# The last memory value slab behind the mixer's output, and the weight splits around the norms

## What is computed

```python
def first_block(x, mem, ...):
    for l in range(DEPTH):                       # DEPTH = 2
        a = hybrid_mixer(rms_norm(x, pre_mix_g[l]), positions, rel_bias, w_in[l], ..., w_mix_out[l])
        x = x + rms_norm(a, post_mix_g[l])
        c = memory_cross_attention(rms_norm(x, pre_xattn_g[l]), rms_norm(mem, mem_g[l]),
                                   w_xq[l], w_xk[l], w_xv[l], w_xo[l])
        x = x + rms_norm(c, post_xattn_g[l])
        hdn = jnp.square(jax.nn.relu(rms_norm(x, pre_mlp_g[l]) @ w_up[l]))
        x = x + rms_norm(hdn @ w_down[l], post_mlp_g[l])
    return x
```

## Time and profile before

| | us |
|---|---|
| median of three runs | 1433.41 |
| lowest and highest | 1430.36, 1434.37 |
| the profiled execution | 1432.31 |
| its span in the trace | 1430.5 |
| TensorE busy | 1352.4 (95%) |
| VectorE busy | 826.6 (58%) |
| ScalarE busy | 661.4 (46%) |

### The profile page before, as it was taken

How to read it: one execution, slowest core, us unless ns; L and a number is a source line. 1 busy time by engine, 2 the same in 40 slices (tenths; PEclk the granted TensorE clock), 3 DMA queues, 4 the chain that set the end, 5 groups by cost and what they waited for, 6 DMA issues and landing times.

```text
span 1430.5 us, 23851 instructions
## 1 busy us (share of the span) xinstructions
PE 1352.4 (95%) x10479; PEld 1298.9 (91%) x10479; DVE 826.6 (58%) x874; ACT 661.4 (46%) x934; POOL 85.3 (6%) x65
## 2 busy tenths in 40 slices
PE   4998999999999999899999999999989998999998
PEld 3997988989999999798898999999888897899998
DVE  5467436566654475743665665437848765666542
ACT  4354435455544444543444554434445544455432
POOL 3000002020000000000202000001100100000000
PEclk7999999999999999999999999999989999999999
DMA  6724234334655533414434365555333122356553
GB/s 190 222 77 148 81 126 148 118 118 147 196 188 189 184 119 93 147 52 155 148 98 138 121 204 183 200 189 150 118 125 119 52 96 89 99 172 200 179 195 101
DMA packets 195574, 202.94 MB, mean 142 GB/s; under 512 B 5716, under 2 KB 191847, under 8 KB 195471
## 3 DMA queue, kind: packets, MB, share of 16 engines
q1 hardware_dynamic: 192704, 194.82, 42.1%
q0 software_dynamic: 2464, 5.99, 1.5%
q10 hardware_dynamic: 303, 0.61, 0.1%
HBM read 200.33 MB, written 3.16 MB: 142 GB/s over the span
## 4 chain that ended last, share of the span: by engine, by line
PE 76%; DVE 11%; ACT 8%; issue 3%; DMA 2%; POOL 0%; ACTq 0%; DVEq 0%; POOLq 0%
PE bank L561 13%; PE bank L562 13%; PE bank L563 13%; PE bank L2083 6%; PE bank L2085 6%; PE bank L2087 6%; DVE w_lo L525 4%; ACT w_hi L515 3%; PE bank L602 2%; PE bank L603 2%; PE bank L604 2%; DVE head_sq L1547 1%; PE bank L1945 1%; PE bank L1923 1%; PE bank L1976 1%
## 5 line engine op out<-in xcount | busy, mean ns | idle before, releaser
L525 DVE TENSOR_TENSOR w_lo<-raw,w_hi 128x2048 fp32r<-128x2048 f32 (+7 forms) x210 | 424.1, 2029 | 429.3 <-ACT w_hi L515 429.0
L515 ACT ACTIVATE w_hi<-raw 128x2048 fp32r<-128x2048 f32 (+7 forms) x210 | 354.8, 1704 | 455.0 <-PE bank L563 190.5
L561 PE MATMUL bank<-act_hi,w_hi 128*128 128x256 f32 x1096 | 312.8, 285 | 0.0
L563 PE MATMUL bank<-act_hi,w_lo 128*128 128x256 f32 x1096 | 310.1, 283 | 0.0
L562 PE MATMUL bank<-act_lo,w_hi 128*128 128x256 f32 x1096 | 310.1, 283 | 0.0
L2083 PE MATMUL bank<-h_hi,w_hi 128*128 128x256 f32 x768 | 212.2, 276 | 0.0
L2085 PE MATMUL bank<-h_lo,w_hi 128*128 128x256 f32 x768 | 212.0, 276 | 0.0
L2087 PE MATMUL bank<-h_hi,w_lo 128*128 128x256 f32 x768 | 212.0, 276 | 0.0
L561 PEld LDWEIGHTS bank<-act_hi,w_hi 128*128 128x128 f32 x1096 | 210.3, 192 | 0.6 <-DVE act_lo L1764 0.3
L562 PEld LDWEIGHTS bank<-act_lo,w_hi 128*128 128x128 f32 x1096 | 210.3, 192 | 0.3
L563 PEld LDWEIGHTS bank<-act_hi,w_lo 128*128 128x128 f32 x1096 | 210.3, 192 | 0.0
(11 more groups left out here) (333 smaller groups left out, 2265.2 us busy)
## 6 DMA issues: line engine op xcount, KB each, us to landing
raw<-in_w_up_dram SPq DMA_DIRECT2D x32, 1024.0 KB, 5.4
raw<-in_w_down_dram SPq DMA_DIRECT2D x32, 1024.0 KB, 4.8
raw<-in_w_ff_dram SPq DMA_DIRECT2D x32, 1024.0 KB, 5.3
raw<-in_w_in_dram SPq DMA_DIRECT2D x23, 1024.0 KB, 5.3
raw<-in_w_xk_dram SPq DMA_DIRECT2D x8, 1024.0 KB, 4.8
raw<-in_w_xv_dram SPq DMA_DIRECT2D x8, 1024.0 KB, 4.9
raw<-in_w_mix_out_dram SPq DMA_DIRECT2D x8, 1024.0 KB, 4.8
raw<-in_w_xq_dram SPq DMA_DIRECT2D x8, 1024.0 KB, 4.8
```

The costliest lines, as they stand in the source:

```text
L515: ins = act.activation(d, r, ACT.Copy)
L525: ins = dve.tensor_tensor(d, r, h.bitcast(F32), ALU.subtract)
L561: pe.matmul(o, stat_hi, mov_hi, start=first, stop=False)
L563: return pe.matmul(o, stat_lo, mov_hi, start=False, stop=last)
```

## The change

**The value slab.** Slabs are renumbered: 16 to 18 are values, 19 to 22 the mixer's output, and 23 is the last value slab. TensorE goes from `ot` 2 and 3 straight to mixer slab 19, of which it multiplies the upper half (k 4 to 7) first, with a wait on `o_lo` 2, then waits for `o_lo` 4 and does the lower half. Behind slab 22 the step `values` does the first 9 matmuls of slab 23 (tile 0, k 0 to 2), then comes `stat` 2, then `values_rest` with the other 39; the dummy matmuls ahead of pair 24 go from 10 to 4. ScalarE copies the bank xv3 behind the eight scaled tiles instead of ahead of the mixer's banks.

**The splits around the norms.** `branch_out` no longer splits a slab ahead of its last bank. Behind the mixer slab 25 is split between the last bank's copy and the root, and slab 26 behind the scaled tiles, on both engines. Behind the cross attention's output slab 34, and behind the down slabs slab 66, are split behind the scaled tiles. In the second block slabs 25 and 29 are split behind the scaled tiles instead of ahead of the last update of x.

The tables of sources and banks follow the numbers and are left out below, as are the callers of `half_slab` with their new last argument.

```diff
      ("slab", 16), ("turn", 9), ("pv", 8), ("turn", 10), ("pv", 9), ("slab", 17), ("turn", 11), ("pv", 10),
-     ("pv", 11), ("slab", 18), ("ot", 2), ("ot", 3), ("slab", 19)]
-    + [("slab", s) for s in range(20, 24)] + [("stat", 2), ("pair", 24), ("stat", 3), ("slab", 26),
+     ("pv", 11), ("slab", 18), ("ot", 2), ("ot", 3)]
+    + [("slab", s) for s in range(19, 23)] + [("values", 23), ("stat", 2), ("values_rest", 23), ("pair", 24), ("stat", 3), ("slab", 26),
      ("scores", 12), ("scores", 13), ("slab", 27), ("turn", 12), ("turn", 13), ("scores", 14), ("scores", 15),
...
+FIRST_VALUES = 3
+
 WARM = {("pair", 0): ("z0", 9), ("turn", 0): ("turn0", 1), ("pv", 0): ("o0", 3), ("pv", 5): ("scores6", 4),
-        ("slab", 16): ("xv0", 6), ("pv", 7): ("xv0", 2), ("pv", 11): ("xv2", 3), ("pair", 24): ("xq0", 10),
+        ("slab", 16): ("xv0", 6), ("pv", 7): ("xv0", 2), ("pv", 11): ("xv2", 3), ("pair", 24): ("xq0", 4),
         ("pair", 32): ("up0", 10), }
...
-        def half_slab(pe, layer, s, o, src_hi, src_lo, half):
+        def half_slab(pe, layer, s, o, src_hi, src_lo, half, opens):
...
                     dst = o[:, T * m:T * m + T]
-                    pe.matmul(dst, wh[:, k, c], src_hi[:, k], start=k == 0 and m == 0, stop=False, skip_group_check=True)
+                    pe.matmul(dst, wh[:, k, c], src_hi[:, k], start=opens and k == 4 * half and m == 0, stop=False, skip_group_check=True)
                     pe.matmul(dst, wh[:, k, c], src_lo[:, k], start=False, stop=False, skip_group_check=True)
-                    ins = pe.matmul(dst, wl[:, k, c], src_hi[:, k], start=False, stop=k == 7, skip_group_check=True)
-            if half:
+                    ins = pe.matmul(dst, wl[:, k, c], src_hi[:, k], start=False,
+                                    stop=not opens and k == 4 * half + 3, skip_group_check=True)
+            if not opens:
                 ins.then_inc(sig["slab_used"], 1)
...
                     for c in range(per_bank):
-                        if (s + c) + 3 <= 66:
+                        if (b, c) != (3, per_bank - 1):
                             split_hi(act, layer, s + c + 3)
...
                 split_hi(act, layer, 18)
-                for b in range(4):
-                    if b == 3:
-                        o_part(layer, 2, 0, 0)
-                        o_part(layer, 3, 0, 1)
+                for b in range(3):
                     split_hi(act, layer, 19 + b)
...
                         turned_out(layer, 9 + 2 * b)
-                branch_out(layer, 2, 20, 0)
+                o_part(layer, 2, 0, 0)
+                o_part(layer, 3, 0, 1)
+                branch_out(layer, 2, 19, 0)
+                split_hi(act, layer, 25)
                 root_of(layer, 2, "stat2", T)
+                act.wait_ge(sig["slab_used"], value("slab_used", layer, 24))
                 scaled_hi(layer, 16, x_t, act_hi, G_PRE_X, square=2,
                           src_ready=lambda k: act.wait_ge(sig["x_new"], value("x_new", layer, k + 1)))
+                act.activation(vx[:, :, 3 * T:4 * T], halves(bank("xv3")[:, :]), ACT.Copy).then_inc(sig["xkv_evac"], 1)
+                split_hi(act, layer, 26)
                 split_hi(act, layer, 27)
...
                           src_ready=lambda k: act.wait_ge(sig["x_new"], value("x_new", layer, 8 + k + 1)))
+                split_hi(act, layer, 34)
                 root_of(layer, 5, "stat5", T)
...
                           src_ready=lambda k: act.wait_ge(sig["x_new"], value("x_new", layer, 16 + k + 1)))
+                split_hi(act, layer, 66)
...
             scaled_hi(DEPTH, 16, x_t, act_hi, N_MEM, square=1, gains=g_2,
-                      src_ready=updated(0, [[22], [23], [24], [25]]))
+                      src_ready=updated(0, [[22], [23], [24], []]))
+            split_hi(act, DEPTH, 25)
             root_of(DEPTH, 1, "stat1", T)
...
             scaled_hi(DEPTH, 24, x_t, act_hi, N_FFN, square=2, gains=g_2,
-                      src_ready=updated(4, [[], [28], [], [29]]))
+                      src_ready=updated(4, [[], [28], [], []]))
+            split_hi(act, DEPTH, 29)
             root_of(DEPTH, 2, "stat2", T)
...
                 split_lo(dve, layer, 22)
-                for s in range(23, 27):
+                for s in range(23, 26):
                     split_lo(dve, layer, s)
                 residual(layer, 2, 0, 0, G_POST_MIX, 16, G_PRE_X)
+                split_lo(dve, layer, 26)
                 split_lo(dve, layer, 27)
...
                 o_rest(layer, 7, 4, 1)
-                for s in range(31, 35):
+                for s in range(31, 34):
                     split_lo(dve, layer, s)
                 residual(layer, 4, 1, 4, G_POST_X, 24, G_PRE_MLP)
+                split_lo(dve, layer, 34)
                 inverse_root(layer, 5, rstd[:, 0:T], root[:, 0:T])
                 hidden_up(layer, 33, 35)
-                for s in range(51, 67):
+                for s in range(51, 66):
                     split_lo(dve, layer, s)
...
                 residual(layer, 6, 2, 8, G_POST_MLP, 32, 0, g_next)
+                split_lo(dve, layer, 66)
...
             for b in range(4):
-                split_lo(dve, DEPTH, 22 + b)
+                if b < 3:
+                    split_lo(dve, DEPTH, 22 + b)
                 update(b, "w", 0, "slab_used", 20 + b)
...
             rests(3, 16, N_MEM)
+            split_lo(dve, DEPTH, 25)
             inverse_root(DEPTH, 1, rstd[:, 0:T], root[:, 0:T])
...
                     update(b, "mo", 4, "slab_used", 26 + b // 2)
-                    split_lo(dve, DEPTH, 28 + b // 2)
+                    if b == 1:
+                        split_lo(dve, DEPTH, 28)
                 if b:
...
             rests(3, 24, N_FFN)
+            split_lo(dve, DEPTH, 29)
             inverse_root(DEPTH, 2, rstd[:, 0:T], root[:, 0:T])
...
                         ins.then_inc(sig["first_bank"] if i == 0 else sig["slab_used"], 1)
-                elif s in (7, 8) or 16 <= s < 20:
+                elif s in (7, 8) or 16 <= s < 19:
                     rows_slab(pe, layer, s, open_bank(pe, layer, names[0]), act_hi, act_lo)
...
                             pe.wait_ge(sig["act_lo"], value("act_lo", layer, 8 + k + 1))
-                    elif s == 20:
+                    elif s == 19:
+                        pe.wait_ge(sig["o_lo"], value("o_lo", layer, 2))
+                        half_slab(pe, layer, s, b, o_hi, o_lo, 1, True)
                         pe.wait_ge(sig["o_lo"], value("o_lo", layer, 4))
-                    from_o = 20 <= s < 24 or 28 <= s < 32
+                        half_slab(pe, layer, s, b, o_hi, o_lo, 0, False)
+                        return
+                    from_o = 20 <= s < 23 or 28 <= s < 32
                     columns_slab(pe, layer, s, b, *((o_hi, o_lo) if from_o else (act_hi, act_lo)), ready=wait)
...
                 pe.wait_ge(sig["o_lo"], value("o_lo", layer, 6))
-                half_slab(pe, layer, s, open_bank(pe, layer, slab_banks(s)[0][0]), o_hi, o_lo, 0)
+                half_slab(pe, layer, s, open_bank(pe, layer, slab_banks(s)[0][0]), o_hi, o_lo, 0, True)
...
                 pe.wait_ge(sig["o_lo"], value("o_lo", layer, 8))
-                half_slab(pe, layer, s, bank(slab_banks(s)[0][0]), o_hi, o_lo, 1)
+                half_slab(pe, layer, s, bank(slab_banks(s)[0][0]), o_hi, o_lo, 1, False)
+
+            def values_of(layer, s, o, tiles):
+
+                wh, wl = w_view(layer, s, 256)
+                for i, k in tiles:
+                    t = slice(P * i, P * i + P)
+                    ins = products3(pe, o[:, T * i:T * i + T], act_hi[:, k, t], act_lo[:, k, t], wh[:, k], wl[:, k],
+                                    k == 0, k == 7)
+                return ins
+
+            def values(layer, s):
+                o = open_bank(pe, layer, slab_banks(s)[0][0])
+                pe.wait_ge(sig["slab_lo"], value("slab_lo", layer, s + 1))
+                values_of(layer, s, o, [(0, k) for k in range(FIRST_VALUES)])
+
+            def values_rest(layer, s):
+                tiles = [(0, k) for k in range(FIRST_VALUES, 8)] + [(1, k) for k in range(8)]
+                values_of(layer, s, bank(slab_banks(s)[0][0]), tiles).then_inc(sig["slab_used"], 1)
-            steps = {"half": half, "rest": rest_of, "slab": slab, "pair": pair, "stat": stat, "kpe": kpe, "scores": scores, "turn": turn, "pv": pv, "ot": turn_o}
+            steps = {"values": values, "values_rest": values_rest, "half": half, "rest": rest_of, "slab": slab, "pair": pair, "stat": stat, "kpe": kpe, "scores": scores, "turn": turn, "pv": pv, "ot": turn_o}
             for layer in range(DEPTH):
```

16 lines of the change are left out of this document (10 added, 6 removed).

## The result

| | before | after |
|---|---|---|
| median (us) | 1431.88 | 1425.48 |
| lowest and highest | 1430.21, 1434.37 | 1419.22, 1426.24 |
| runs | 7 | 7 |
| profiled execution | 1432.31 | 1420.13 |
| its span | 1430.5 | 1418.3 |

What follows compares the result with a forecast made beforehand. TensorE was taken to bound the kernel, 76% of the chain that ended last. Savings of 6.1 + 2.5 + 4.3 + 2.1 = 15.0 us, less 2.0 for the clock, gave 1420.4 from 1433.41, predicted as 1420, range 1416 to 1426.

Steps and rivals of the forecast that it cites:

- faster: The whole kernel measures faster than before, beyond the 0.3% that can't be told from no change: chance 0.95.
- the base: Time of the kernel before that the gain is taken from: median 1433.41 us of three runs, profiled execution 1432.31.
- Steps 1 and 2: Mixer's output to the next pair: mixer done 3.6 us earlier, reciprocal 0.5 us later, in each layer.
- Step 3: Slab 26's split moved behind the scaled tiles: 0.1 us lost per layer, later loads and splits hidden by 2 us.
- slower rival: Late xo loads hold ScalarE ahead of the exponentials in both layers, making the kernel slower: 1436 us, chance 0.02.
- Step 4: Cross attention's output: without slab 34's split the sum runs through, 1.24 us off per layer, 2.5 us in all.
- Step 5: Down slabs: without slab 66's split the reciprocal comes 2.16 us sooner per layer, 4.3 us in all.
- Step 6: Second block: without the splits of slabs 25 and 29 two pair gaps, 1.12 and 0.97 us, close: 2.1 us off.
- Step 7: Clock behind the new 2.2 us gap before the mixer slab's lower half: 2 us lost, bounds nothing to 6 us.
- the likeliest case: The forecast itself: one of the two new gaps is answered by a low clock, 2 us lost; chance 0.38.
- low clock at both: Low clock behind both new gaps, or a long stretch: 4 to 6 us lost, 1423 to 1424.5 us; chance 0.20.
- the row at 1215: A 2.19 us gap before 1215.23 us, followed by a granted clock of 0.50, taken as a sure fall.

Runs made afterwards that it cites:

- e1: The changed kernel again with no edit: 1426.73 us, ratio 0.9968.
- e4: The changed kernel with four dummy matmuls between the upper and lower half of the mixer's first output slab: 1419.68 us, ratio 0.9922.
- e2: The changed kernel with the later splits undone at the cross attention's output, the down slabs and in the second block: 1430.23 us, ratio 0.9996.
- e5: The changed kernel with 16 dummy matmuls in the second block's gate slab: 1424.37 us, ratio 0.9954.
- e9: The changed kernel with 6 dummy matmuls in the second block's gate slab: 1427.86 us, ratio 0.9974.
- e7: The changed kernel with the upper halves of slabs 19 and 20 both ahead of their lower halves: 1418.22 us, ratio 0.9914.
- e8: The changed kernel with two upper halves first and 16 dummy matmuls in the second block's gate slab: 1423.2 us, ratio 0.9949.
- e11: The changed kernel with two upper halves first and 6 dummy matmuls in the second block's gate slab: 1420.06 us, ratio 0.9925.

## Why the prediction came out as it did

The median of 1425.48 lies inside the range of 1416 to 1426, at its upper edge, and "faster" was right. That the median lies inside is in part luck: eight more runs of the same kernel, e1, have theirs at 1426.73, outside. The forecast was 13.0 us off against the base, measured are 6.4. The forecast of 1420 is the time of the profiled execution, which is luck too, as the sum below shows, and 5.5 us below the median. By its steps, against the profiles:

| step | forecast | measured |
|---|---|---|
| 1 and 2, slab 19 to pair, clock aside, a layer | -3.1 | -3.04 (e4), -3.03 in layer 1 |
| 3, pair to the next output norm, a layer | +0.1 | +0.1 (e4) to +0.3 (after) |
| 4, cross attention's norm, a layer | -1.24 | -0.81 |
| 5, down norm, a layer | -2.16 | -1.87 |
| 6, second block's two pairs | -2.1 | -2.6 |
| 7, clock behind the new gaps, both | +2 | +3.8 |

- **Steps 1 and 2 held.** The gap is 1.98 us (forecast 2.2), and the mixer's output takes 24.1 us on TensorE in e4, where the clock is kept (forecast 24.25); ScalarE's last square comes 24.4 us behind its start, since it waits for GpSimd's add there as well. The pair starts 9.7 us after that square, as forecast, with a last gap of 0.61.
- **Step 3 held.** The first exponential starts at 264.44 us, a microsecond ahead of the forecast, the splits of slabs 28 and 29 at 258.44 and 261.20 (forecast 259 and 262), and the transposes at 267.10 don't wait. The cost of the moved split is a few tenths. The slower rival had nothing to work with.
- **Step 4 was mis-sized by 0.4 us a layer.** I let ScalarE have its last square and the table load done beside the sum. But the square itself waits for GpSimd (`2.56 <-POOL`), as the rows above show, so copy and table load stand behind GpSimd's add in the same chain: 305.24 to the root at 307.64, 2.40 us, where TensorE's sum alone would have given 1.92.
- **Step 5** is short by 0.2 to 0.3: the reciprocal follows the sum's start by 2.59 us, not 2.44, and the stage ends 1.87 us sooner.
- **Step 6** gave more than the gaps: from the pair's first matmul to its sum 12.97 us became 11.58, and 12.83 became 11.59.
- **Step 7 failed on its size, and the likeliest case was the wrong one.** I took one answer out of two gaps. Both were answered in all five profiles that have this gap (after, e1, e2, e5, e9), ten of ten, each with 3.4 us at 0.50 or so, and none in e4, e7, e8 and e11, where it is filled. e4 prices one answer at 1.9 us by the layer stage. That is my rival "low clock at both", at the small end of its 4 to 6 us. I had also called the row at 1215 a sure fall. It is none: the same gap of 2.19 us stands in all 14 profiles and was answered in nine.
- The Trainium skill (TensorE: Matmul & The Clock Gate, "What's actually happening") has the gate run free of the kernel, from which I drew that the same gap may be answered or not. At the new gap no run here shows that: ten of ten, though in all ten the clock fell 1.0 to 1.4 us after TensorE resumed, so they were much alike. Elsewhere the traces agree: the gap of 2.19 us just named was answered in one execution of the changed kernel (e1) and not in the other; the down norm's wait of 1.68 us was answered in both layers of e2 and in neither of the kernel before, and the longest low stretch of the second block's opening was 10.2 us in one execution of the changed kernel and 27.3 us in another.

In sum the first two profiles give 7.5 us in the layers and 2.6 us in the pairs, 10.1 us. The profiled execution shows 12.2: 1.7 us of it is a low stretch of 3.4 us at 1216 us that this execution did not have, and 0.4 came ahead of the layers. The medians show 6.4 and, in e1, 3.8. **The step that the prediction lacked is this one**: it took the second block's time from one profile as given. The opening there took 187.1 to 193.4 us in the eight profiles without dummies in the gate slab. That accounts for the 6 us between the two profiles of the changed kernel. In these eight the opening's time goes with the sum of its low clock: 187.1 to 187.2 us with 17 to 20 us of it, 189.1 with 24, 191.7 to 193.4 with 27 to 38. The runs without a profile point the same way. By the mean clocks (what is missing to 1, twice, times the span) the clock was low for about 85 us in e1 and for 63 us in the kernel before beside it; the new gaps account for 6.8 of the 22 us more. Why the changed kernel is found more often in its long form than the kernel before (its mean clock over the runs is 0.967 to 0.977, that of before mostly 0.976 to 0.981) stays open: the change shifts the whole second block in time by 7.5 to 7.9 us, and does nothing else to the opening; the runs without a profile don't tell which stretch they lost. Lastly, the median of before fell by 1.5 us with more runs, which the base had as 1433.41.

## What to carry over

- Filling a stall is worth more than its length: behind a TensorE gap of 2 us nearly as much again (1.9 us) was lost to the clock, so a move that opens a gap should bring work to put into it (here the next slab's upper half), and dummies if there is none; dummies on the path itself cost their full length, twice that at half clock.
- When a stall shrinks, look at what ends next: here a GpSimd add of 2.9 us was level with TensorE once the split ahead of the last square was gone, and took 1.2 of the next 2 us.
- Cut the profiles at landmarks and compare stage by stage, and take a second profile of the same kernel: each layer repeated to 0.3 us, while a stage that nobody had touched moved by 6. Cut that stage further before aiming at its most visible part: the longest low stretch was worth 1.5 of the 6 us.
